# The order of a sliding-window attention stage: one pass for each pair of heads, and two banks for each block pair

## The reference, cut to what matters

```python
def sliding_window_attention(q, k, v, sinks):   # 16 query heads, 2 key heads, 64 wide, window 128
    def block(args):                            # 128 queries against 256 keys
        qi, i = args
        ...
        s = jnp.einsum('bqhgd,bkhd->bhgqk', qi.astype(jnp.float32), kb) * scale + bias
        m = jnp.maximum(jnp.max(s, axis=-1, keepdims=True), sink)
        p = jnp.exp(s - m)
        denom = jnp.sum(p, axis=-1, keepdims=True) + jnp.exp(sink - m)
        return jnp.einsum('bhgqk,bkhd->bqhgd', p / denom, vb)
```

## Time and profile before

| | us |
|---|---|
| median of three runs (1888.08 to 1888.32) | 1888.32 |
| the profiled execution's own time | 1887.79 |
| its span | 1886.0 |
| TensorE busy in the span | 1869.4 (99%) |
| VectorE busy | 1176.4 (62%) |
| ScalarE busy | 787.8 (42%) |
| GpSimd busy | 144.3 (8%) |
| the second mixer's loop, from its first scores to the end of its last values | 580.78 to 683.37 |

### The profile page before, as it was taken

How to read it: one execution, slowest core, us unless ns; L and a number is a source line. 1 busy time by engine, 2 the same in 40 slices (tenths; PEclk the granted TensorE clock), 3 DMA queues, 4 the chain that set the end, 5 groups by cost and what they waited for, 6 DMA issues and landing times.

```text
span 1886.0 us, 24346 instructions
## 1 busy us (share of the span) xinstructions
PE 1869.4 (99%) x8998; PEld 1497.1 (79%) x8998; DVE 1176.4 (62%) x1824; ACT 787.8 (42%) x1182; POOL 144.3 (8%) x106
## 2 busy tenths in 40 slices
PE   8999999999999999999999999999999999999999
PEld 6767888888887788888888887888777788888887
DVE  5786677357646866763566498675655667743762
ACT  4365443133435654342334343422566544322441
POOL 2011100000021010000000101121211020000000
PEclk9999999999999999999999999999999999999999
DMA  6112222322231122223232322445333122233222
GB/s 217 68 50 70 103 90 74 114 103 89 84 106 57 48 88 90 89 89 112 89 103 80 118 89 92 145 139 185 131 116 112 63 94 89 78 100 112 89 78 100
DMA packets 38306, 185.99 MB, mean 99 GB/s; under 512 B 4385, under 2 KB 4769, under 8 KB 23505
## 3 DMA queue, kind: packets, MB, share of 16 engines
q1 hardware_dynamic: 38080, 184.90, 28.8%
q10 hardware_dynamic: 144, 0.02, 0.0%
HBM read 176.42 MB, written 8.49 MB: 98 GB/s over the span
## 4 chain that ended last, share of the span: by engine, by line
PE 92%; DVE 4%; ACT 2%; DMA 1%; issue 0%; SPq 0%; DVEq 0%; ACTq 0%
PE banks L738 55%; PE banks L1227 22%; PE banks L789 5%; PE banks L1141 1%; PE banks L1166 1%; PE banks L1152 1%; PE banks L1271 1%; PE banks L1112 1%; DVE w_lo L1892 1%; PE banks L1300 1%; DVE tmp L2276 1%; PE banks L1283 1%; PE banks L1240 1%; ACT w_hi L1377 1%; DMA raw<-weights 1%; PE banks L904 1%
## 5 line engine op out<-in xcount | busy, mean ns | idle before, releaser
L738 PE MATMUL banks<-xn_hi,w_hi 128*128 128x512 f32 x1240 | 481.1, 392 | 6.5 <-ACT w_hi L1856 5.6
L738 PE MATMUL banks<-xn_hi,w_lo 128*128 128x512 f32 x1240 | 478.1, 390 | 0.0
L738 PE MATMUL banks<-xn_lo,w_hi 128*128 128x512 f32 x1240 | 478.1, 390 | 0.0
L1377 ACT ACTIVATE w_hi<-raw 128x2048 fp32r<-128x2048 f32 (+2 forms) x134 | 228.3, 1704 | 228.5 <-PE banks L738 194.4
L1892 DVE TENSOR_TENSOR w_lo<-raw,w_hi 128x2048 fp32r<-128x2048 f32 (+2 forms) x134 | 273.8, 2043 | 46.7 <-ACT w_hi L1377 46.2
L738 PEld LDWEIGHTS banks<-xn_hi,w_hi 128*128 128x128 f32 x1240 | 233.3, 188 | 57.3 <-ACT w_hi L1856 5.6
L738 PEld LDWEIGHTS banks<-xn_lo,w_hi 128*128 128x128 f32 x1240 | 233.3, 188 | 49.7 <-issue 1.4
L738 PEld LDWEIGHTS banks<-xn_hi,w_lo 128*128 128x128 f32 x1240 | 233.3, 188 | 48.8
L1439 ACT ACTIVATE tmp<-scaled_h,par 128x512 f32<-128x512 f32 x132 | 100.5, 809 | 349.9 <-DVE scaled_h L1937 349.9
L1937 DVE TENSOR_TENSOR scaled_h<-banks,token_rs 128x512 f32<-128x512 f32 x132 | 85.0, 686 | 186.3 <-PE banks L738 166.1
L1227 PE MATMUL banks<-xn_hi,w_hi 128*128 128x512 f32 x400 | 161.2, 403 | 0.6 <-DVE big L1987 0.6
(11 more groups left out here) (270 smaller groups left out, 2547.5 us busy)
## 6 DMA issues: line engine op xcount, KB each, us to landing
raw<-weights SPq DMA_DIRECT2D x115, 1024.0 KB, 4.9
raw<-weights SPq DMA_DIRECT2D x24, 768.0 KB, 4.4
raw<-weights SPq DMA_DIRECT2D x24, 640.0 KB, 4.0
big<-scratch SPq DMA_DIRECT2D x40, 256.0 KB, 4.3
att<-scratch SPq DMA_DIRECT2D x16, 256.0 KB, 4.3
scratch<-stage SPq DMA_DIRECT2D x12, 256.0 KB, 4.3
scratch<-con SPq DMA_DIRECT2D x12, 256.0 KB, 2.3
out<-x SPq DMA_DIRECT2D x4, 512.0 KB, 4.0
```

The costliest lines, as they stand in the source:

```text
L738: return pe.matmul(psum[:, 2 * p + m, :], w[:, at_:at_ + P], x_part(k), start=start, stop=stop)
L1377: act.activation(w_hi[:, sl], raw[:, sl], ACT.Identity).then_inc(hi_done, 1)
```

## The change

The scores and the turned probabilities of a round now lie in the same two banks: 4 and 5 for even rounds, 6 and 7 for odd ones. `scores(r)` waits for the copies of round r - 2 and no longer for the maxima of round r - 1; `turn` has no wait for a copy of its own. The loop of each engine runs over pairs, with no lag inside a pair: TensorE does both scores of a pair with the last pair's values between and behind them, the norm, the even fill, the even turn, the odd fill, the odd turn. VectorE does both `maxima`, the last pair's `output`, then for each round `evacuate`, `finish`, `scaled` (odd), `alibi`, `lo_piece`. ScalarE does both `exps`, `high`, `norm_job`, then for each round `copy` and `hi_piece`.

```diff
--- before.py
+++ after.py
@@ -450,6 +450,9 @@
 
         def c_hi_chunk(it):
             return chunk(big_r, 12 + it)
+
+        def c_score_bank(m, r):
+            return 4 + 2 * (r % 2) + m
 
         C_UNIT_STEPS = unit_steps(C_FILL, {})
 
@@ -1262,13 +1265,13 @@
                     it = r // 2
                     if r % 2 == 0:
                         pe.wait_ge(c_qk, it + 2)
-                    if r:
-                        pe.wait_ge(c_max, 4 * r)
+                    if r >= 2:
+                        pe.wait_ge(c_copied, 2 * r - 2)
                     for b, i, w in c_blocks(r):
                         lo = max(i - 1, 0) * P
                         for m in range(2):
                             h = 64 * m
-                            last = pe.matmul(psum[:, 4 + m, 256 * b + 256 - w:256 * b + 256], qn[it % 2][h:h + 64, i * P:(i + 1) * P],
+                            last = pe.matmul(psum[:, c_score_bank(m, r), 256 * b + 256 - w:256 * b + 256], qn[it % 2][h:h + 64, i * P:(i + 1) * P],
                                              kn[0][h:h + 64, lo:lo + w], start=(b == 0), stop=(b == 1), skip_group_check=True)
                             if b == 1:
                                 last.then_inc(c_scored, 1)
@@ -1276,11 +1279,9 @@
                 def turn(r):
                     for m in range(2):
                         pe.wait_ge(c_fin, 2 * r + m + 1)
-                        if r:
-                            pe.wait_ge(c_copied, 2 * r - 1 + m)
                         for b, i, w in c_blocks(r):
                             for j in range(256 - w, 256, P):
-                                last = pe.transpose(psum[:, 6 + m, 256 * b + j:256 * b + j + P], c_prob(m, r, b)[:, j:j + P], ident)
+                                last = pe.transpose(psum[:, c_score_bank(m, r), 256 * b + j:256 * b + j + P], c_prob(m, r, b)[:, j:j + P], ident)
                         last.then_inc(c_pt, 1)
 
                 def values(r):
@@ -1328,16 +1329,20 @@
                 last.then_inc(c_turned_v, 1)
                 norm_job(1)
                 woven(q, 32, 48, xh, xl)
-                for r in range(C_ROUNDS + 2):
-                    if r < C_ROUNDS:
-                        scores(r)
-                    fill(r)
-                    if 1 <= r <= C_ROUNDS:
-                        turn(r - 1)
-                    if r % 2 == 0 and r // 2 + 1 < C_PAIRS:
-                        norm_job(1 + r // 2 + 1)
-                    if r >= 2:
-                        values(r - 2)
+                for it in range(C_PAIRS + 1):
+                    for r in (2 * it, 2 * it + 1):
+                        if it < C_PAIRS:
+                            scores(r)
+                        if it:
+                            values(r - 2)
+                    if it + 1 < C_PAIRS:
+                        norm_job(it + 2)
+                    fill(2 * it)
+                    if it < C_PAIRS:
+                        turn(2 * it)
+                    fill(2 * it + 1)
+                    if it < C_PAIRS:
+                        turn(2 * it + 1)
                 for s in (o + 2, o + 3):
                     woven(s, 0, 48, lambda k: c_hi_chunk(4 + k), lambda k: c_lo_chunk(4 + k), out_ready(4))
 
@@ -1610,7 +1615,7 @@
                         act.wait_ge(c_pt, 2 * r + m + 1)
                         if m == 0 and r >= 2:
                             act.wait_ge(c_pv, r - 1)
-                        act.activation(c_slot(m, r)[:, c0:T], psum[:, 6 + m, c0:T], ACT.Identity).then_inc(c_copied, 1)
+                        act.activation(c_slot(m, r)[:, c0:T], psum[:, c_score_bank(m, r), c0:T], ACT.Identity).then_inc(c_copied, 1)
 
                 def high(it):
                     act.wait_ge(c_pv, 2 * it + 2)
@@ -1625,21 +1630,22 @@
                 act.wait_ge(c_turned_v, 1)
                 act.activation(vtok[0], psum[:, 2, :], ACT.Identity).then_inc(c_v, 1)
                 norm_job(1)
-                for r in range(C_ROUNDS + 2):
-                    if r % 2 == 0 and r >= 4:
-                        high(r // 2 - 2)
-                    if r % 2 == 1 and r // 2 + 1 < C_PAIRS:
-                        norm_job(1 + r // 2 + 1)
-                    if r < C_ROUNDS:
-                        exps(r)
-                    if 1 <= r <= C_ROUNDS:
-                        copy(r - 1)
-                    for s, g0, n in C_FILL:
-                        if n < 4 and r == g0:
-                            hi_piece(s + 1, 0, 1)
-                        elif n >= 4 and g0 <= r < g0 + 2:
-                            hi_piece(s + 1, r - g0, 2)
-                high(C_PAIRS - 1)
+                for it in range(C_PAIRS + 1):
+                    if it < C_PAIRS:
+                        exps(2 * it)
+                        exps(2 * it + 1)
+                    if it:
+                        high(it - 1)
+                    if it + 1 < C_PAIRS:
+                        norm_job(it + 2)
+                    for r in (2 * it, 2 * it + 1):
+                        if it < C_PAIRS:
+                            copy(r)
+                        for s, g0, n in C_FILL:
+                            if n < 4 and r == g0:
+                                hi_piece(s + 1, 0, 1)
+                            elif n >= 4 and g0 <= r < g0 + 2:
+                                hi_piece(s + 1, r - g0, 2)
                 hi(o + 3, 0)
                 for n in range(2):
                     if n:
@@ -2189,7 +2195,7 @@
                         dve.wait_ge(c_scored, 2 * r + m + 1)
                         for b, i, w in c_blocks(r):
                             dve.tensor_tensor_reduce(
-                                out=c_prob(m, r, b)[:, 256 - w:256], in0=psum[:, 4 + m, 256 * b + 256 - w:256 * b + 256],
+                                out=c_prob(m, r, b)[:, 256 - w:256], in0=psum[:, c_score_bank(m, r), 256 * b + 256 - w:256 * b + 256],
                                 in1=c_bias[it % 2][:, 256 * m + 256 - w:256 * m + 256], scale=-1.0,
                                 scalar=neg_sink[:, 2 * it + m:2 * it + m + 1], op0=ALU.add, op1=ALU.min,
                                 accum_out=neg_max[:, 2 * i + m:2 * i + m + 1]).then_inc(c_max, 1)
@@ -2224,31 +2230,32 @@
                 evacuate(q, 0)
                 sink_columns(0)
                 evacuate(q, 1)
-                for r in range(C_ROUNDS + 2):
-                    if 1 <= r <= C_ROUNDS:
-                        finish(r - 1)
-                    if r % 2 == 0 and 0 < r < C_ROUNDS:
-                        sink_columns(r // 2)
-                    if r < C_ROUNDS:
-                        maxima(r)
-                    if r % 2 == 1 and r // 2 + 1 < C_PAIRS:
-                        scaled(1 + r // 2 + 1)
-                    if r % 2 == 0 and r >= 4:
-                        output(r // 2 - 2)
-                    if r // 2 + 1 < C_PAIRS:
-                        alibi(r // 2 + 1, r % 2)
-                    for s, m, done in C_UNIT_STEPS:
-                        if done == r - 1 and done >= 0:
-                            evacuate(s, m)
-                    for s, g0, n in C_FILL:
-                        if n < 4 and r == g0 + 1:
-                            lo_piece(s + 1, 0, 1)
-                        elif n >= 4 and g0 + 1 <= r < g0 + 3:
-                            lo_piece(s + 1, r - g0 - 1, 2)
+                for it in range(C_PAIRS + 1):
+                    if it < C_PAIRS:
+                        if it:
+                            sink_columns(it)
+                        maxima(2 * it)
+                        maxima(2 * it + 1)
+                    if it:
+                        output(it - 1)
+                    for r in (2 * it, 2 * it + 1):
+                        for s, m, done in C_UNIT_STEPS:
+                            if done == r - 1 and done >= 0:
+                                evacuate(s, m)
+                        if it < C_PAIRS:
+                            finish(r)
+                        if r % 2 == 1 and it + 1 < C_PAIRS:
+                            scaled(it + 2)
+                        if it + 1 < C_PAIRS:
+                            alibi(it + 1, r % 2)
+                        for s, g0, n in C_FILL:
+                            if n < 4 and r == g0 + 1:
+                                lo_piece(s + 1, 0, 1)
+                            elif n >= 4 and g0 + 1 <= r < g0 + 3:
+                                lo_piece(s + 1, r - g0 - 1, 2)
                 for s, m, done in C_UNIT_STEPS:
                     if done == C_ROUNDS + 1:
                         evacuate(s, m)
-                output(C_PAIRS - 1)
                 lo(o + 3, 0)
                 for n in range(2):
                     if n:
```

## The result

The changed kernel takes 1901.11 us, median of four runs (1900.31 to 1902.03), against 1888.32 before on the same chip (1888.08 to 1888.44): ratio 1.007, 95% interval 1.0058 to 1.0083. It is slower by 12.8 us; forecast were 13.0 and 1901.3.

What follows compares the result with a forecast made beforehand. TensorE's own work bounds the kernel, so its added waits count: 9.0 + 4.7 - 0.66 = +13.0 us on the profiled execution, 1900.8, plus 0.53 to the runs' median: 1901.3 us; range 1894 to 1909.

Steps and rivals of the forecast that it cites:

- TensorE's own work: Same matmuls in the same nine groups per pair, only neighbours change: 0 us, with 2.9 us either way for group switches.
- the rival "Faster": No waits at the turns and fills 0.18 cheaper behind a norm or turn: 1884.7 us; chance 0.04.
- The chain in a plain pair: Even turn waits for VectorE's normalisation, queued behind the output that awaits ScalarE's high part: 1.37 us in pairs 1 to 5.
- Pairs 6 and 7, without GpSimd beside them: Even turns there, with the normalisation taking 1.01 instead of 1.80: idle time of 0.58 us and 1.53 us.
- The weight pieces: VectorE's half waits for ScalarE's late piece, delaying the next maxima: 1.9 us in pairs 1 and 6, 0.9 in pair 3.
- Sum of the waits: New TensorE idle time in the loop: 9.0 us from the even turns' chain and 4.7 from the weight pieces.
- The 0.66: TensorE's only old idle time, the first output-projection fill awaiting the fourth pair's output: 0.66 us, expected to go.
- The clock as a rival: TensorE falls to its lower clock after about 3 us idle in pairs 1 and 6: 1906.5 us; chance 0.10.
- The banks: Scores wait for copies of the round two before, which end earlier; the waits removed never ended late: 0 us.

Runs made afterwards that it cites:

- e3: Changed kernel with VectorE's even normalisation moved ahead of the last pair's output and, in odd rounds, ScalarE's weight piece ahead of the copy: 1884.80 us.
- e2: Changed kernel with one move on ScalarE: in odd rounds the weight piece comes ahead of the copy of the turned probabilities: 1894.65 us.
- e8: e3 plus eight unneeded additions on VectorE ahead of one even normalisation, to make TensorE idle about 3.5 us: 1890.43 us.
- e6: Changed kernel with one move on VectorE: the evacuation of the fill's bank comes behind the even normalisation, the output stays ahead of it: 1893.38 us.
- e7: e3 plus six unneeded additions on VectorE ahead of pair 4's even normalisation, to make TensorE idle about 2 us: 1888.20 us.
- e5: Changed kernel's order of work with the old banks and waits: all scores in banks 4 and 5, turned probabilities in 6 and 7: 1910.05 us.
- e1: Changed kernel with one move on VectorE: the even normalisation comes ahead of the last pair's output and of the evacuation: 1887.41 us.

## Why the prediction was right, point by point

- **TensorE's own work: 0, with 2.9 either way.** Mis-sized. e3 has neither idle time nor slow matmuls, and takes 121.45 us from the first scores to the next stage (580.53 to 701.98) against 124.48: 3.0 less, of which 0.66 is the wait of the earlier trace rows. So the switches give 2.4, inside the bound, on its lower side. This is what the rival "Faster" asked for, the normalisation ready at every turn, and it gains 2.9 us in the medians, for 3.6 forecast under that condition. I counted switches and not which they were: an even turn directly ahead of a fill is cheaper than one ahead of values, and a fill ahead of which stands the norm is cheaper than one behind scores.
- **The chain in a plain pair: 1.37.** Right in every link (above) to 0.05. The loss of a pair is 13.41 - 11.86 = 1.55, since TensorE's own work is shorter than I took it. The profile calls only 1.22 of it idle time: idle time is counted from the modelled end of the last matmul, and the turn behind a wait takes 0.76 to the next fill (617.10 to 617.86) instead of 0.58 (609.68 to 610.26 in e3). So each stop costs some 0.3 more than its bracket says.
- **Pairs 6 and 7, without GpSimd beside them.** Right: in e2, where no weight piece disturbs them, they idle 0.43 and 1.31, forecast 0.58 and 1.53.
- **The weight pieces: 1.9, 0.9 and 1.9.** Right: e2 took 4.4 us of idle time away, forecast 4.7.
- **Sum of the waits: 13.7.** The changed kernel's loop is 138.42 - 121.45 = 17.0 longer than e3's; without the 2.6 of the clock, 14.4 are waits, which is the 12.2 of idle time and some 0.3 more at each of the seven stops.
- **The 0.66.** Gone, as said.
- **The clock as a rival, chance 0.10.** In the profiled execution it came in one of its two places. The forecast left it out and was still 0.2 us off the median, because the 2.6 it costs stand against the 2.4 of the switches. The mechanism was right; that the figure is so close is luck of two terms that cancel. Profiled against profiled, as the sum was made, it is 13.8 for 13.0. The 3 us of idle time were rightly foreseen for pair 1 (pair 6 had 2.22; by the forecast's own terms it was to have 0.58 + 1.9 = 2.5, not the about 3 that it says), and so was the price of a fall, though it was taken near the upper end of what the kernel's start allowed; the chance was too low. The one row that spoke against it, matmuls at full rate behind 0.66, said little of a stretch four times as long. The Trainium skill (TensorE: Matmul & The Clock Gate, Why this matters for your kernels), which warns of idle gaps between bursts of matmuls in mid-kernel, was the better guide here. The traces agree with it in pair 1 (3.01) and in e8 (3.54), and differ on shorter gaps: the clock fell behind 1.64 and 2.09 too (e6, e7), and in e5 behind one stretch of 2.84 and not behind another.
- **The banks: no cost, no gain.** Right for the new order, in that no wait for them was seen; but the text let it seem as if they were idle in the change. e5 shows what they are for: the pair order without them is some 9 us slower still.

What stays open: on what it depends whether a stretch of 1.6 to 3 us brings the clock down. By the mean clock of its runs the same program did and did not (e7, e6), so not on the stretch's length alone; no run here tells more.

## What to carry to other kernels

When steps are moved closer together, list for the engine that bounds the kernel what must be ready at each of its waits, and walk each other engine's queue in its new order up to that point: a step that is ready may stand behind one that is not. Here a change that brought two useful things (cheaper neighbours, room for both scores) was 13 us slower for two calls that stood behind a wait for another engine, and 3 us faster once both had changed places. Put what the bounding engine wants next ahead of what it wants a pair later.

## What the runs showed of the hardware

- TensorE can fall to its lower clock behind one idle stretch of 1.64, 2.09, 2.84, 3.01 or 3.54 us in an otherwise full stage, and stays there for 3 to 6 us (seven matmuls at 0.63 in e7, a whole turn and fill in the changed kernel). Behind other stretches of 2.04, 2.22 and 2.84 it stayed up. A fall added 2.6 us to the price of the stall in the changed kernel and 2.4 in e8, and runs of one kernel spread: 1900.31 to 1902.03 in four, against 1884.41 to 1885.11 in ten of e3.
- The matmuls right behind a stretch can still run at full rate and the slow ones come 1.6 us later (e7).
- A short stop of TensorE costs more than its idle time in the profile: 1.55 us of a pair for 1.22 (changed kernel against e3).
- The SBUF operation of VectorE that meets GpSimd's square of 512 columns (1.04 to 1.08 long) takes longer: the normalisations of a round 1.80 instead of 1.01 (before and after), a weight piece 2.06 instead of 1.23 (e1). Moving the evacuation that releases it moves who pays.
